# Two column blocks of the output projection accumulated head by head inside the attention loop

## The chip, the core and the metric

One core of one Trainium2 chip runs the whole program. The metric is the device time in microseconds (us), the median over several executions. Engines: PE is the matmul engine, ACT the scalar engine, DVE the vector engine, POOL GpSimd, SP the engine whose queue issues the weight loads.

## What is computed

Two layers of a decoder trunk for 256 tokens of width 2048, all in float32. Each layer is a mixer and a gated ConvFFN, each behind a norm with a learned modulation and added to x through a gate:

```
x = x + gate * mixer(modulate(norm(x)))      # layer 0: NSA (8 heads) and MLA (8 heads)
x = x + gate * conv_ffn(modulate(norm(x)))
x = x + gate * mixer(modulate(norm(x)))      # layer 1: DSA (16 heads, top-k mask)
x = x + gate * conv_ffn(modulate(norm(x)))
mixer(h) = concat(heads) @ w_out             # (256, 2048) @ (2048, 2048)
```

An NSA head is the gated sum of three attentions (compressed, selected, window). The gate and the modulation come from `silu(c) @ ada_w + ada_b`, whose weights are streamed too.

## The kernel before

The program has four sub-layers, n = 0 to 3: even mixer, FFN, odd mixer, FFN. The change touches n = 0 and n = 2.

**Matmuls by weights.** A projection is worked off in units. A unit is 128 rows by 512 columns of a weight, 256 KB, loaded by SP into one of 8 slots of `ring` (`matrix`, L417, by `unit`, L411, which waits until the slot's last unit is used). For precision each factor is split in two: ACT rounds the unit (`high`, L1046) into `ring_hi`, DVE takes the remainder (`low`, L1443) into `ring_lo`, and PE forms hi x hi, lo x hi and hi x lo (`rows_block`, L774): six matmuls of 128x512 per unit, over two tiles of 128 tokens. The left factor is split in the same way, `hT` into `hT_hi` (ACT) and `hT_lo` (DVE, `low_hT`, L1460). All four streams are queues written out by hand; each engine runs its own in order, and they meet at semaphores that count (`hi_ok`, `lo_ok`, `unit_used`, ...).

**Attention.** `pe_attention` (L601), ACT's `attention` (L1159) and DVE's (L1584) run one loop over units: for the even mixer 24 NSA units, three per head (cmp, slc, win), then 8 MLA units; for the odd mixer 16 DSA units, one per head. Step n of the loop holds on PE: query transposes for unit n+1 if it begins a head, logits of n, transposes of the probabilities of n-2, values of n-3. On ACT: copy of the queries, exponentials of n, scaling of n-1, copy of the transposed probabilities of n-2. On DVE: bias, mask and row maximum of n (`logits`), the reciprocal of the sums of n-1 (`weights`), the copy of a finished head (unit n-4) into `hT` (L1623), and in every second step one late unit of the modulation (`rest_unit`, L1422: one operation over 128x2048). PSUM has eight banks; logits (S_B), transposes (T_B), values (O_B) and queries (Q_B) have two each and turn over them, so all eight are used (L588). Before attention starts ACT and DVE have split the first six units of `ev_out` or `od_out` (L1279, L1710).

**Output projection.** After attention all engines wait for the last head, and `out_side` (PE L817, ACT L1121, DVE L1511) follows: ACT and DVE split `hT` pair by pair, and PE works off four blocks of 512 columns, 16 units each, in banks 0 to 3, two banks per block. Between block 0 and block 1 PE spreads the gate row over the partitions (`gate_rows`, L810, banks 4 to 7), which ACT copies back. After each block DVE adds the gated result to x (`residual`, L1498: four operations over 128x512), and ACT squares x for the next norm. The remaining late units of the modulation are spread over blocks 1 and 2 (`more`, L1527). Before the last block PE sums the modulation (`column_sums`, L739), which waits for the last of these units.

## Time and profile before

| | us |
|---|---|
| median of 3 runs | 2169.94 (2161.24 to 2180.1) |
| the profiled execution | 2174.66 |
| its span | 2173.0 |
| busy: PE, DVE, ACT, POOL | 1938.5, 1569.0, 1090.7, 129.2 |
| even attention | 377.7 to 485.0 |
| even output projection | 489.0 to 588.4 |
| odd attention | 1444.0 to 1494.5 |
| odd output projection | 1499.5 to 1598.6 |

The span is what the trace covers; the execution's own time is 1.7 us longer. Busy time of PE includes the modelled drain of its pipelined matmuls. The clock column of a window is the mean clock granted to PE, 1.00 for 2.4 GHz.

### The profile page before, as it was taken

What the parts mean: (1) busy time and instruction counts of PE and PEld (TensorE: products, weight loads), DVE (VectorE), ACT (ScalarE), POOL (GpSimd) and SP (SyncE); (2) the same over time, 40 slices, a digit from 0 to 9 for tenths busy, and PEclk for the clock granted to TensorE, in tenths of its full rate; (3) what the DMA queues carried; (4) which work ended last, traced back from release to release, by engine and by line L of the source; (5) the groups of instructions that cost most, each with busy time, mean ns of one, the idle gap of its engine ahead of it and who ended that gap; (6) DMA issues with size and microseconds to landing.
All of it is one profiled execution on the core that took longest, in us unless ns stands there. A gap on an engine that the chain in (4) does not pass through costs nothing.

```text
span 2173.0 us, 35788 instructions
## 1 busy us (share of the span) xinstructions
PE 1938.5 (89%) x11518; PEld 1684.7 (78%) x11518; DVE 1569.0 (72%) x2443; ACT 1090.7 (50%) x2384; POOL 129.2 (6%) x221
## 2 busy tenths in 40 slices
PE   3189978789899999999998999748989999999998
PEld 2068855567699999997777777636779999998787
DVE  4987743765787878887876767687766777778554
ACT  1145625674455455556454555346545555556443
POOL 1210000000100000000010000000000000000000
PEclk9589979799999999999999999669999999999999
DMA  8979965456588878785985998445757677665565
GB/s 326 401 258 342 328 232 161 155 174 216 172 284 272 278 245 280 255 278 188 327 281 187 331 314 308 137 163 203 251 182 226 221 242 223 221 221 171 178 188 178
DMA packets 210837, 521.47 MB, mean 240 GB/s; under 512 B 24945, under 2 KB 38770, under 8 KB 185874
## 3 DMA queue, kind: packets, MB, share of 16 engines
q1 hardware_dynamic: 180578, 316.17, 45.1%
q0 software_dynamic: 28032, 201.44, 25.1%
q10 hardware_dynamic: 2096, 2.12, 0.3%
q8 instruction: 81, 1.33, 0.2%
q14 instruction: 50, 0.41, 0.1%
HBM read 517.52 MB, written 2.12 MB: 239 GB/s over the span
## 4 chain that ended last, share of the span: by engine, by line
PE 77%; DVE 10%; DMA 6%; ACT 3%; issue 3%; SPq 0%; DVEq 0%; ACTq 0%; POOLq 0%
PE ps L794 12%; PE ps L789 12%; PE ps L790 12%; PE ps L860 11%; PE ps L856 11%; PE ps L857 11%; DVE acc L1381 4%; PE ps L916 2%; DMA first_ring<-in_ada_w 2%; PE ps L648 2%; DVE ring_lo L1449 1%; PE ps L908 1%; DMA ring<-in_ffn_w_down 1%; DMA ring<-in_od_w_in 1%; DMA ring<-in_ffn_w_up 1%
## 5 line engine op out<-in xcount | busy, mean ns | idle before, releaser
L1010 ACT ACTIVATE ring_hi<-ring 128x512 fp32r<-128x512 f32 (+1 forms) x1152 | 696.0, 622 | 657.4 <-DMA ring<-in_ffn_w_up 255.1
L1449 DVE TENSOR_TENSOR ring_lo<-ring,ring_hi 128x512 fp32r<-128x512 f32 (+1 forms) x1152 | 741.6, 679 | 373.4 <-ACT ring_hi L1010 371.5
L856 PE MATMUL ps<-hT_hi,ring_hi 128*128 128x256 f32 x2048 | 513.8, 283 | 5.3 <-issue 4.6
L857 PE MATMUL ps<-hT_lo,ring_hi 128*128 128x256 f32 x2048 | 508.7, 280 | 0.0
L856 PEld LDWEIGHTS ps<-hT_hi,ring_hi 128*128 128x128 f32 x2048 | 386.2, 189 | 6.1 <-issue 5.6
L857 PEld LDWEIGHTS ps<-hT_lo,ring_hi 128*128 128x128 f32 x2048 | 388.7, 190 | 0.0
L860 PE MATMUL ps<-hT_hi,ring_lo 128*128 128x256 f32 x2048 | 330.1, 282 | 1.5 <-issue 1.4
L789 PE MATMUL ps<-ring_hi,hT_hi 128*128 128x512 f32 (+2 forms) x768 | 302.0, 394 | 14.5 <-issue 9.4
L790 PE MATMUL ps<-ring_hi,hT_lo 128*128 128x512 f32 (+2 forms) x768 | 301.0, 393 | 0.0
L860 PEld LDWEIGHTS ps<-hT_hi,ring_lo 128*128 128x128 f32 x2048 | 280.1, 188 | 1.9 <-issue 1.6
L1381 DVE SCALAR_TENSOR_TENSOR acc<-aring,cs_now,acc 128x2048 f32<-128x2048 f32 x106 | 249.3, 2352 | 7.1 <-DMA aring<-in_ada_w 1.2
L794 PE MATMUL ps<-ring_lo,hT_hi 128*128 128x512 f32 (+2 forms) x768 | 238.4, 392 | 3.4 <-DVE ring_lo L1449 3.4
L789 PE MATMUL ps<-ring_hi,act_hi 128*128 128x512 f32 x512 | 202.8, 396 | 5.0 <-issue 5.0
L790 PE MATMUL ps<-ring_hi,act_lo 128*128 128x512 f32 x512 | 201.9, 394 | 0.0
L528 POOL DMA_DIRECT2D aring<-in_ada_w x176 | 93.0, 528 | 1597.2 <-DVE acc L1381 1574.8
L789 PEld LDWEIGHTS ps<-ring_hi,hT_hi 128*128 128x128 f32 x768 | 149.0, 194 | 49.4 <-issue 10.3
L1381 DVE SCALAR_TENSOR_TENSOR acc<-aring,cs,acc 128x2048 f32<-128x2048 f32 x70 | 164.6, 2351 | 12.7 <-DMA aring<-in_ada_w 6.0
L790 PEld LDWEIGHTS ps<-ring_hi,hT_lo 128*128 128x128 f32 x768 | 149.0, 194 | 31.5 <-issue 0.5
L794 PEld LDWEIGHTS ps<-ring_lo,hT_hi 128*128 128x128 f32 x768 | 145.9, 193 | 35.0 <-DVE ring_lo L1449 5.4
L794 PE MATMUL ps<-ring_lo,act_hi 128*128 128x512 f32 x512 | 161.6, 397 | 2.7 <-DVE ring_lo L1449 2.7
L1786 DVE SCALAR_TENSOR_TENSOR cbuf<-ps,cw_now,cbuf 128x255 f32<-128x255 f32 (+1 forms) x256 | 123.5, 482 | 18.2 <-ACT cbuf L1010 9.3
L789 PEld LDWEIGHTS ps<-ring_hi,act_hi 128*128 128x128 f32 x512 | 97.1, 190 | 29.0 <-issue 5.9
(205 smaller groups left out, 1662.6 us busy)
## 6 DMA issues: line engine op xcount, KB each, us to landing
aring<-in_ada_w POOLq DMA_DIRECT2D x176, 1024.0 KB, 6.4
ring<-in_ffn_w_up SPq DMA_DIRECT2D x512, 256.0 KB, 2.9
ring<-in_ffn_w_down SPq DMA_DIRECT2D x256, 256.0 KB, 3.2
ring<-in_od_w_in SPq DMA_DIRECT2D x128, 256.0 KB, 4.6
ring<-in_ev_w_in SPq DMA_DIRECT2D x96, 256.0 KB, 5.6
first_ring<-in_ada_w POOLq DMA_DIRECT2D x16, 1024.0 KB, 7.0
ring<-in_ev_w_out SPq DMA_DIRECT2D x64, 256.0 KB, 3.1
ring<-in_od_w_out SPq DMA_DIRECT2D x64, 256.0 KB, 3.2
```

The costliest lines, as they stand in the source:

```text
L528: pool.dma_start(slot, src).then_inc(landed_, 16)
L648: ins = nc.tensor.matmul(ps[:, b, off:off + nk], l, r, start=j == 0, stop=j == len(parts) - 1)
L789: nc.tensor.matmul(o, hi, w_hi[:, k, :], start=start, stop=False)
L790: nc.tensor.matmul(o, lo, w_hi[:, k, :], start=False, stop=False)
L794: ins = nc.tensor.matmul(ps[:, bank + t, 0:n], hi, w_lo[:, k, :], start=False, stop=stop)
L856: nc.tensor.matmul(o[q], hi, hT_hi[:, kt, :], start=start, stop=False, skip_group_check=True)
L857: nc.tensor.matmul(o[q], hi, hT_lo[:, kt, :], start=False, stop=False, skip_group_check=True)
L860: ins = nc.tensor.matmul(o[q], w_lo[:, k, q * P:(q + 1) * P], hT_hi[:, kt, :], start=False, stop=u == KT - 1, skip_group_check=True)
L1010: ins = nc.scalar.activation(out_, in_, f, **kw)
L1381: put(v.scalar_tensor_tensor(acc[:, t, :], slot, col, acc[:, t, :], ALU.mult, ALU.add), ada_used)
L1449: put(v.tensor_tensor(ring_lo[:, g, part], ring[:, g, part], ring_hi[:, g, part].bitcast(F32), ALU.subtract), lo_ok)
L1786: put(v.scalar_tensor_tensor(cb, u, cw_now[:, s, 1 - tap, gv, q:q + 1], cb, ALU.mult, ALU.add), gconv if (gv == 0 and tap == 1) else None)
```

## The change

Blocks 0 and 1 of each mixer's output projection are no longer formed after attention. Their four output tiles live in banks 0 to 3 during the whole attention loop, and head q's part (units 2q and 2q+1: rows of head q, columns of block 0 and of block 1) is added in step last(q)+5. SP loads the units in that order (`paired`). What attention used two banks for it now does in one: S_B, T_B, O_B, Q_B are 4, 5, 6, 7. A head is split straight from bank O: ACT rounds it (`rounded`, first thing in step last+4) into the place of its own queries, DVE subtracts (`remainder`, same step, after logits) into `hT_lo`; `hT` and `hT_hi` aren't used here any more. ACT's highs for head q stand at the end of step last+3, DVE's lows at the end of step last+4. MLA's rotary queries get a turn of their own in bank Q. Blocks 2 and 3 follow attention, in banks 4, 5 and 0, 1; the gate rows are formed two and two, in banks 6 and 7, before and inside block 2; residuals 0 and 1 run during block 2, and all late units of the modulation that are left lie in block 2. The FFN's projections stay as they are, under the name `down`.

```diff
-            narrow("ev_out", ev_w_out[0], KT)
+            paired("ev_out", ev_w_out[0])
...
-        S_B, T_B, O_B, Q_B = 0, 2, 4, 6
+        S_B, T_B, O_B, Q_B = 4, 5, 6, 7
+        SPLIT_AT, PRODUCT_AT = 3, 5
+        def head_at(att, n, late):
+            return att.qh[n - late] if n - late in att.last_of else None
...
-                if n >= 2:
-                    pe.wait_ge(att.l_ok.handle, n - 1)
+                if n >= 1:
+                    pe.wait_ge(att.l_ok.handle, n)
...
-                if n >= 2:
-                    pe.wait_ge(att.pt_ok.handle, n - 1)
+                if n >= 1:
+                    pe.wait_ge(att.pt_ok.handle, n)
...
-                if first and q >= 2:
-                    pe.wait_ge(att.o_out.handle, q - 1)
+                if first and q >= 1:
+                    pe.wait_ge(att.o_out.handle, q)
...
+                rotary(n + 1)
+                q = head_at(att, n, PRODUCT_AT)
+                if q is not None:
+                    pe.wait_ge(att.o_out.handle, q + 1)
+                    for b in range(2):
+                        product(q, b)
...
+            def heads_out(name, n, att):
+                left = parts_of_heads(att)
+                pe_attention(pe, lane, att, head_product(name, left))
+                gate_rows(n, range(0, 2))
+                rows_block(name, 2 * KT, KT, NB, 4, left, part=(0, 6))
+                pe.wait_ge(gate_ok.handle, 4 * n + 2)
+                gate_rows(n, range(2, 4))
+                rows_block(name, 2 * KT, KT, NB, 4, left, part=(6, KT))
+                pe.wait_ge(gate_ok.handle, 4 * n + 4)
+                column_sums(n + 1)
+                pe.wait_ge(res_out.handle, 4 * n + 1)
+                rows_block(name, 3 * KT, KT, NB, 0, left, part=(0, 6))
+                column_turn(n + 1)
+                rows_block(name, 3 * KT, KT, NB, 0, left, part=(6, KT))
...
+            def heads_out(name, n, next_name):
+                highs(name, 2 * KT, 2 * KT + 4)
+                gate_copies(n, 1, range(0, 2))
+                highs(name, 2 * KT + 4, 2 * KT + 8)
+                gate_copies(n, 2, range(2, 4))
+                run(None, root[:, :], ones[:, 0:1], ACT.Sqrt)
+                highs(name, 2 * KT + 8, 2 * KT + 12)
+                for b in range(2):
+                    act.wait_ge(res_out.handle, 4 * n + b + 1)
+                    x_squares(b)
+                highs(name, 2 * KT + 12, 3 * KT + AHEAD)
...
+                for n in range(len(units) + LAG + 2):
+                    rounded(n)
                     queries(n + 1)
...
+                    rotary(n + 1)
+                    q = head_at(att, n, SPLIT_AT)
+                    if q is not None:
+                        highs(name, 2 * q, 2 * q + 2)
...
-                highs("ev_out", 0, AHEAD)
-                attention(EVA)
+                attention(EVA, "ev_out")
...
+            def heads_out(name, n, next_name):
+                late = len(MOD_REST[n]) - rest_at[n]
+                def more(u0, u1):
+                    for u in range(u0, u1):
+                        low(name, u)
+                        if due(u - 2 * KT, KT, late):
+                            rest_unit(n)
+                more(2 * KT, 2 * KT + 6)
+                residual(name, n, KT, 0)
+                more(2 * KT + 6, 2 * KT + 10)
+                residual(name, n, KT, 1)
+                more(2 * KT + 10, 3 * KT)
+                lows(name, 3 * KT, 3 * KT + 2)
+                residual(name, n, KT, 2)
...
-                for n in range(len(units) + 5):
+                for n in range(len(units) + LAG + 3):
+                    if 0 <= n - 1 < len(units):
+                        weights(n - 1)
                     if n < len(units):
                         logits(n)
-                    if 0 <= n - 1 < len(units):
-                        weights(n - 1)
-                    if 0 <= n - 4 < len(units):
-                        output(n - 4)
+                    remainder(n)
+                    q = head_at(att, n, SPLIT_AT + 1)
+                    if q is not None:
+                        lows(name, 2 * q, 2 * q + 2)
                     if n % every == every - 1:
                         rest_unit(n_sub)
...
-                lows("ev_out", 0, AHEAD)
                 dve.wait_ge(bias_ok.handle, 8)
-                attention(EVA, 0, 2)
+                attention(EVA, "ev_out", 0, 2)
```

## Rows read from the trace of the kernel before

**Rows 1.** The page, part 1: busy us (share of the span) xinstructions.
```profile
PE 1938.5 (89%) x11518; PEld 1684.7 (78%) x11518; DVE 1569.0 (72%) x2443; ACT 1090.7 (50%) x2384; POOL 129.2 (6%) x221
```

**Rows 2.** Windows, even side: PE, PEld, DVE, ACT, POOL busy, PEclk, DMA, GB/s.
```profile
377.70:398.00 20.30, 15.66 (x56) 12.15 (x57) 14.51 (x43) 12.28 (x43) 1.06 (x2) 0.55 0.30 104
398.00:448.50 50.50, 39.62 (x192) 30.95 (x190) 38.01 (x124) 33.12 (x128) 4.75 (x9) 0.83 0.54 180
448.50:485.00 36.50, 33.99 (x194) 25.19 (x194) 23.24 (x58) 26.77 (x88) 3.17 (x6) 0.95 0.44 156
...
489.00:540.20 51.20, 51.15 (x203) 40.24 (x204) 30.44 (x42) 22.94 (x41) 1.23 (x3) 0.94 0.61 209
540.20:588.40 48.20, 47.14 (x214) 36.29 (x213) 31.01 (x43) 24.19 (x42) 5.08 (x5) 1.00 0.61 205
```

**Rows 3.** Windows of odd attention and its first two blocks, same columns.
```profile
1444.00:1458.50 14.50, 11.44 (x58) 10.22 (x59) 10.74 (x29) 9.80 (x31) 1.05 (x2) 0.76 0.30 92
1458.50:1494.50 36.00, 29.61 (x212) 25.88 (x210) 30.27 (x79) 29.18 (x98) 3.17 (x6) 1.00 0.53 184
...
1499.50:1551.30 51.80, 51.72 (x205) 40.48 (x206) 32.71 (x43) 23.13 (x40) 1.75 (x4) 0.94 0.64 214
```

**Rows 4.** Waits in the NSA stretch: total us, times, longest.
```profile
PE ps L662 <- ACT L L1010: 13.6, 10, 2.8
```

**Rows 5.** Timeline of one MLA step on PE: start us, us, engine line op.
```profile
456.02 0.38 PE L615 MATMUL ps<-con,side 128*64 128x128 f32 x2
...
459.71 0.38 PE L615 MATMUL ps<-con,side 128*64 128x128 f32 x2
```

**Rows 6.** Timeline of odd attention, PE and DVE.
```profile
1459.88 0.42 DVE L1604 CUSTOM_DVE_ANT_0 L<-ps,bias 128x256 f32<-128x256 f32 x1 [0.85 <-PE ps L648]
...
1461.42 0.38 PE L621 MATMUL ps<-con,wide 128*128 128x128 f32 x2
...
1462.51 0.33 PE L662 MATMUL ps<-con,L 128*128 128x128 f32 x1
...
1463.72 0.38 PE L621 MATMUL ps<-con,wide 128*128 128x128 f32 x2
```

**Rows 7.** Timeline of DVE: copies of heads 0 and 6.
```profile
399.76 0.42 DVE L1623 COPY hT<-ps 128x256 f32<-128x256 f32 x1
...
442.03 0.42 DVE L1623 COPY hT<-ps 128x256 f32<-128x256 f32 x1
```

**Rows 8.** Timeline of PE in the second block: one unit.
```profile
530.82 0.62 PE L794 MATMUL ps<-ring_lo,hT_hi 128*128 128x512 f32 x2
...
532.21 0.62 PE L794 MATMUL ps<-ring_lo,hT_hi 128*128 128x512 f32 x2
```

**Rows 9.** Timeline: PE's first matmul of the projection.
```profile
489.05 0.76 PE L789 MATMUL ps<-ring_hi,hT_hi 128*128 128x512 f32 x1 [4.16 <-issue]
```

**Rows 10.** Timeline of ACT in odd attention.
```profile
1466.73 0.50 ACT L1010 ACTIVATE L<-L,nmx 128x256 f32<-128x256 f32 x1
...
1467.61 0.79 ACT L1010 ACTIVATE L<-L,rw 128x256 f32<-128x256 f32 x2
1468.30 0.47 ACT L1010 ACTIVATE PT<-ps 128x384 f32<-128x384 f32 x1
1468.67 0.46 ACT L1010 ACTIVATE qT<-ps,gs 128x256 f32<-128x256 f32 x1
```

**Rows 11.** Groups by line, even projection: busy, mean ns, idle before.
```profile
L1449 DVE TENSOR_TENSOR ring_lo<-ring,ring_hi 128x512 fp32r<-128x512 f32 x58 | 38.0, 688 | 30.3 <-ACT ring_hi L1010 30.1
L1010 ACT ACTIVATE ring_hi<-ring 128x512 fp32r<-128x512 f32 x60 | 37.0, 630 | 47.1 <-DMA ring<-in_ev_w_out 45.3 <-DMA ring<-in_ffn_w_up 1.6
L1381 DVE SCALAR_TENSOR_TENSOR acc<-aring,cs,acc 128x2048 f32<-128x2048 f32 x5 | 11.8, 2353 | 0.5
L1506 DVE TENSOR_TENSOR rtmp<-ps,acc 128x512 f32<-128x512 f32 x7 | 4.8, 688 | 7.0 <-PE ps L794 6.6
```

**Rows 12.** Timeline of DVE at the start of even attention.
```profile
377.44 3.69 DVE L1449 TENSOR_TENSOR ring_lo<-ring,ring_hi 128x512 fp32r<-128x512 f32 x6
```

More of the change, by code:

```diff
@@ L447, in narrow, with paired @@
                         matrix(PLAN[name] + units * b, w, units, i * (2 * NB) + b * NB, NB, i * (2 * units))
+            def paired(name, w):
+                for kt in range(KT):
+                    for b in range(2):
+                        g = PLAN[name] + 2 * kt + b
+                        unit(g, g, w[kt * P:(kt + 1) * P, b * NB:(b + 1) * NB], ring[:, g % RING, :])
+                for b in range(2, 4):
+                    matrix(PLAN[name] + KT * b, w, KT, b * NB, NB)
             def up(name, w):
@@ L693, in pe_attention @@
             queries(0)
-            for n in range(len(units) + LAG + 1):
+            for n in range(len(units) + PRODUCT_AT):
                 queries(n + 1)
@@ L786, in rows_block @@
                         for t in range(ST):
-                            o, rows_ = ps[:, bank + t, 0:n], slice(t * P, (t + 1) * P)
-                            hi, lo = (part(u * UK + k)[:, rows_] for part in left)
+                            o = ps[:, bank + t, 0:n]
+                            hi, lo = (x(u * UK + k, t) for x in left)
                             nc.tensor.matmul(o, hi, w_hi[:, k, :], start=start, stop=False)
@@ L808, in in_proj, with gate_rows @@
                 rows_block(name, 2 * KT * pairs, KT, cols - 2 * pairs * NB, 0, h_parts)
-            def gate_rows(n):
+            def gate_rows(n, js=range(4)):
                 pe.wait_ge(ada_used.handle, first_mod(n) + GATE_UNITS[n])
-                for j in range(4):
-                    ins = nc.tensor.matmul(ps[:, 4 + j, :], ones[:, :], acc[:, 2, j * NB:(j + 1) * NB], start=True, stop=True)
+                for j in js:
+                    ins = nc.tensor.matmul(ps[:, (6 + j % 2) if n % 2 == 0 else 4 + j, :], ones[:, :], acc[:, 2, j * NB:(j + 1) * NB],
+                                           start=True, stop=True)
@@ L815, in gate_rows, with head_product, product @@
                 lane.done(ins, gate_red)
-            def out_side(name, n, units, left):
-                rows_block(name, 0, units, NB, 0, left, pairs_before=PAIRS_BEFORE[n, "out"])
-                if n % 2 == 1:
-                    pe.wait_ge(up_pair.handle, 32 * (n // 2 + 1))
+            def head_product(name, left):
+                def product(kt, b):
+                    at, start, stop = 2 * kt + b, kt == 0, kt == KT - 1
+                    w_hi, w_lo = (x[:, (PLAN[name] + at) % RING, :] for x in (ring_hi, ring_lo))
+                    pe.wait_ge(hi_ok.handle, nth(name, at, 0))
+                    for t in range(ST):
+                        hi, lo = (x(kt, t) for x in left)
+                        nc.tensor.matmul(ps[:, 2 * b + t, :], hi, w_hi, start=start, stop=False)
+                        nc.tensor.matmul(ps[:, 2 * b + t, :], lo, w_hi, start=False, stop=False)
+                    pe.wait_ge(lo_ok.handle, nth(name, at, 0))
+                    for t in range(ST):
+                        ins = nc.tensor.matmul(ps[:, 2 * b + t, :], left[0](kt, t), w_lo, start=False, stop=stop)
+                    lane.done(ins, unit_used)
+                return product
@@ L826, in out_side @@
                     if b == 0 or n == 3:
[L827 removed]
+                        rows_block(name, FT * (2 + b), FT, NB, 2 * b, act_parts)
                     else:
@@ L1135, in out_side, with down @@
+            def down(name, n, next_name):
+                units = FT
+                for u in range(units // 2):
+                    act.wait_ge(up_pair.handle, 32 * (n // 2) + turns_for(u))
+                    run(h_hi, act_hi[:, 2 * u:2 * u + 2, :], act_pair(u), ACT.Copy)
+                    if 2 * u >= AHEAD:
+                        highs(name, 2 * u, 2 * u + 2)
+                    if u % 2 == 1 and u < 8:
+                        up_tile(n // 2, 28 + u // 2, u // 2, 1)
                 highs(name, units, units + AHEAD)
-                act.wait_ge(gate_red.handle, n + 1)
@@ L1137, in out_side @@
-                for j in range(4):
-                    run(gate_ok, acc[:, 2, j * NB:(j + 1) * NB], ps[:, 4 + j, :], ACT.Copy)
+                gate_copies(n, 1)
                 if n < 3:
@@ L1169, in queries, with rotary @@
                         act.wait_ge(att.s_ok.handle, att.last_of[q - 2] + 1)
-                    bank = Q_B if kind == "mla" else Q_B + q % 2
                     if kind == "mla":
-                        run(None, qpT[:, q % 2, :], ps[0:ROPE, Q_B + 1, 0:S], ACT.Copy, scale=(HD + ROPE) ** -0.5)
                         run(None, knT[:, q % 2, :], ps[:, Q_B, S:2 * S], ACT.Copy, scale=prm[:, ROWS["nope_g"][0] + 1:ROWS["nope_g"][0] + 2])
                     g = {"dsa": 1, "mla": 2}.get(kind, 0)
-                    run(att.q_ok, qT[:, q % 2, :], ps[:, bank, 0:S], ACT.Copy, scale=gs[:, g:g + 1])
+                    run(att.q_ok, qT[:, q % 2, :], ps[:, Q_B, 0:S], ACT.Copy, scale=gs[:, g:g + 1])
+                def rotary(n):
+                    if n < len(units) and units[n][0] == "mla":
+                        act.wait_ge(att.r_raw.handle, units[n][1] + 1)
+                        run(att.r_ok, qpT[:, qh[n] % 2, :], ps[0:ROPE, Q_B, 0:S], ACT.Copy, scale=(HD + ROPE) ** -0.5)
                 def exps(n):
```

193 lines of the change are left out of this document (111 added, 82 removed).

## The prediction

> **What bounds the kernel now.** The page comes first: the matmul engine, PE, is busy 89% of the span [rows 1], so a gain must come out of time in which PE stands still or runs slowly. Next, the stages by window. Even attention runs from 377.7 to 485.0 us and odd attention from 1444.0 to 1494.5 us. Each output projection follows with four blocks, the first two ending at 540.2 and 1551.3 us. Over the blocks PE is busy 47 to 51 us of each 48 to 52 [rows 2, 3], so there the matmul work itself is the bound. Over attention PE is busy 15.66 of 20.3, 39.62 of 50.5 and 33.99 of 36.5 us (even), 11.44 of 14.5 and 29.61 of 36.0 us (odd). The clock granted is 0.55 in the first stretch and 0.83 in the second; the two levels are 1.2 and 2.4 GHz, so a third of the second stretch ran at the lower one. The holes are therefore in the 24 NSA units (three per head); with the 8 MLA units PE hardly stands.
>
> The waits say what ends the holes: in the NSA stretch PE waits 13.6 us, ten times, for ACT's scaled probabilities [rows 4]. At 2.4 GHz one step of the pipeline takes PE 3.69 us in MLA [rows 5] and 2.30 us in odd attention, from one head's query transposes (1461.42) to the next's (1463.72) [rows 6]. The NSA steps come from DVE's copies of finished heads: head 0 at 399.76, head 6 at 442.03, so 7.05 us per head [rows 7].
>
> **What the work costs.** A unit of a block takes 1.39 us (530.82 to 532.21) [rows 8]; a head's product, two units, takes 2.77 us, and 16 heads 44.3 us per projection. The same matmuls run either way, so moving them saves only what falls into PE's holes, plus the hand-over. Today PE stands 4.16 us before the first unit at 489.05 [rows 9] and the first two blocks have a mean clock of 0.94, which is about 3 us of slow running in 51.2 [rows 2]. The odd side is alike [rows 3]. So 7 us per projection go for certain, because the product follows attention with no rounding of the whole hT in between. Beside each product ACT gets two highs (0.63 busy, about 0.55 apart: 1.1 us) and the rounding of the head, bounded by 0.36 (the step from PT at 1468.30 to qT at 1468.67, [rows 10]) and 0.63 (a high); I take 0.37. DVE gets two lows, 0.688 each less overlap: 1.3 us, and the remainder, which replaces the copy of about 0.42 and costs the same (bounds 0.4 and 0.69) [rows 7, 11].
>
> **Even attention, step by step.** Each engine runs its queue in order. I followed the waits of the new code, with durations from the steps shown [rows 5, 6, 10]. PE's odd step divides into queries and logits, 1.09 (1461.42 to 1462.51), and transposes and values, 1.21 (to 1463.72); by the number of operations I split these into 0.22 and 0.87, 0.5 and 0.7. NSA's parts are a little shorter, having no mask matmuls. Per unit: DVE's two logits reductions 0.65 (0.42 for the wider, at 1459.88, and about half of it for the other), ACT's exponentials 0.89 (1466.73 to 1467.61), its scaling 0.70, the copy 0.37, a semaphore about 0.08. Two things are new. With one bank O, PE's first values of a head wait for DVE's remainder of the head before, which waits for ACT's rounded copy, and in ACT's queue this stands behind the two highs. With one bank T, PE's transposes wait for one more copy. From the end of one product to the end of the next, in NSA: queries 0.22, PE logits 0.93, DVE logits 0.72, exponentials 0.98, scaling 0.70, copy 0.30, highs 1.10, rounded 0.37, remainder 0.49, values 0.70, logits 0.73, transposes 0.44, values 0.64, product 2.77: 11.1 us. Against 7.05 + 2.77 = 9.8 us apart, each such head loses 1.3 us instead of gaining. In MLA the chain is remainder 0.5, values 0.66, rotary 0.22, product 2.77, queries 0.66, logits 2.3, DVE logits 0.7: 7.8 us against 3.69 + 2.77 = 6.5.
>
> The sum: six steps before the first product 22 us; 6 heads x 11.1 = 66.6; the eight MLA steps 51 (four at 7.8, the earlier ones with two products and two waits 19.8); the tail with five products 17.5; less 1.2, because six lows of 3.69 us no longer stand ahead of DVE's first logits [rows 12]. That is 155.9, and the gate rows (four matmuls, 3.6 us by both orders) make 159.5. Before, 377.7 to 540.2 is 162.5. So 3 us come out here, at full clock.
>
> But before, a third of the NSA stretch was at 1.2 GHz, and PE still has holes of 1 to 1.5 us in that chain. If the clock drops there, a product costs up to 2.77 more: bounds 0 and 6 x 2.77 = 17 us. I take 5, by the third (17/3). The Trainium skill, TensorE: Matmul & The Clock Gate, A second HAM failure mode, says that cycling PSUM banks with small idles between matmul groups makes the clock swing; by it the upper bound would be the nearer. The rows agree that it swings in this stage: 0.55, 0.83, 0.95 [rows 2].
>
> **Odd attention.** Here every unit is a head, so each step carries a product. The chain: remainder 0.5 after DVE's logits, values 0.66, product 2.77, queries 0.22, logits 1.1, DVE logits 0.65: 5.9 us, against 2.30 + 2.77 = 5.07 of pure PE work. Five steps without product 14.5, then 3.1 + 10 x 5.9 = 62, the tail 21: 97.5, with gate rows 101.1. Before, 1444.0 to 1551.3 is 107.3. So 6 us come out.
>
> **The third block (block 2).** The late units of the modulation (5 even, 6 odd, 2.353 us each on DVE) were spread over two blocks and now lie in one [rows 11]. In its 22.2 us DVE has 16 lows 11, those units 11.8 or 14.1, and two residuals of 4 x 0.688 = 2.7 each: 28 or 31 us. DVE can begin about 5 us ahead, at the tail of attention, but residual 0 waits for the last product, and the ring of 8 units limits the lead. ACT's second gate copies now stand in the middle of the block, and its squares wait for residual 1. I count PE standing 5 us (even) and 7 us (odd), with the column sums behind the last unit; before, the last two blocks together hold PE up 1 us (48.2 - 47.14, [rows 2]). Net loss 4 and 6 us. Bounds for both together: 0 if the lead holds, 18 if there is none (DVE's excess over PE, 6 and 8, and 2 each for the copies).
>
> **Sum.** Even -3 + 5 + 4 = +6, odd -6 + 6 = 0. With the unknowns leaning both ways I take +5 us. The profiled execution took 2174.7 us (span 2173.0), 4.7 above the median of 2169.9; so 2179.7 there, and as a median 2174 to 2175. I say 2174. The measurement can tell about 1%, 22 us; this lies within it.
>
> **Where rules pull.** The Trainium skill, Perfetto Trace Analysis, Optimization Strategy, holds that interleaving stages with different bounds may pay; MLA and odd attention, at 93 and 82% PE, are hardly a different stage. The same page, Matmuls, wants matmul groups to rotate through PSUM banks so that evacuation overlaps; the change takes that away, and what it costs is in the chains above.
>
> **Rivals.** *The holes are filled* (faster): the steps do not lengthen as I chain them, because highs run before ACT is needed and PE, denser, keeps 2.4 GHz. For: PE's holes plus slow running in NSA are large (its busy 55.3 us at a mean clock of 0.75 is 42 us of work at full clock in a stretch of 70.8). Then a head takes 9.3 instead of 11.1 (-11) and keeps the clock (-5), the start at 0.55 improves by 4, and the third blocks stall 3 instead of 12 (-9): -29 from my sum, 2145. Against: ACT is already the releaser of PE [rows 4]. Chance 0.2.
>
> *One bank each is the bound* (slower): the hand-over PE to DVE to ACT to PE through single banks, with 2.353 us modulation units of DVE in its middle, and a clock that falls in the holes. Place: NSA products. Price: the clock term at 17 instead of 5 (+12), two of three such units falling inside the chain, 6 heads x 1 us (+6), and the third blocks at 18 instead of 12 (+6): 2198. It decides from about 13 us per NSA head on. For: PE's wait for ACT [rows 4], and the clock of 0.55 and 0.83 [rows 2]. Chance 0.24.
>
> *The order does not do what it says*: weights arrive late, since two units per 6 to 11 us replace a full ring at the start of the block. Against: 256 KB per unit in a few us and DMA far from full (share 0.30 to 0.54, [rows 2]). Then the products cost more, and it is a part of the second rival. My forecast has 0.56.
>
> **How the numbers follow.** Range: 2146 to 2197. It reaches to the first rival's time and to the second's, so that about half of either's chance, 0.22 in all, lies outside; my sum's own bounds, with the clock term from 0 to 17 and the third blocks from 0 to 18, are 2157 to 2192. Under 2148.2 is faster by over 1%, above 2191.6 slower: 0.20, 0.56, 0.24 come from the three cases.
>
> **What would show it.** Between two products about 11 us in NSA, 7.8 in MLA, 5.9 in odd attention; the waits naming DVE's remainder (hT_lo) ahead of PE's values, and ACT's rounded copy behind highs; a first block end near 542 to 547 and attention with two blocks near 101 us on the odd side; in the third block DVE busy nearly throughout with PE waiting for ring_lo for some us. If NSA products stand 9.5 us apart at clock 1.0, the first rival is right; at 13 and more with a clock at 0.8, the second. Wrong altogether if the hand-over hole of 4 us stays.

## The result and the profile after

The changed kernel takes 2194.7 us (median of four runs, 2186.5 to 2197.8) beside 2170.8 for the kernel before in the same comparison. The ratio is 1.0112, with a 95% interval of 1.0075 to 1.0149: slower, by about 1%, and the interval is clear of no change. The forecast was 2174, with a range of 2146 to 2197. The range holds the time, near its upper end; the case called the likeliest, no change to speak of, is not the one that came.

The page, part 1 (busy us, share of the span, instructions; its span is 2191.0), against [rows 1]:

```profile
PE 1949.1 (89%) x11518; PEld 1684.6 (77%) x11518; DVE 1555.7 (71%) x2427; ACT 1087.9 (50%) x2400; POOL 129.2 (6%) x221
```

PE's share is the same, but it is 11 us busier with the same 11518 instructions, so some of them ran slower. The windows say where (columns as in [rows 2]). Even side: up to the first product, five NSA products, MLA, the tail, blocks 2 and 3. Odd side: up to the first product, the products, blocks 2 and 3:

```profile
375.75:400.96 25.21, 18.46 (x71) 13.82 (x71) 15.16 (x53) 15.17 (x53) 1.58 (x3) 0.64 0.35 116
400.96:469.80 68.84, 56.18 (x223) 43.57 (x221) 38.83 (x109) 35.58 (x125) 3.94 (x8) 0.75 0.44 149
469.80:522.88 53.08, 46.85 (x185) 32.43 (x183) 19.59 (x56) 27.94 (x86) 1.85 (x4) 0.72 0.32 109
522.88:557.70 34.82, 32.81 (x164) 25.71 (x162) 24.52 (x39) 18.43 (x47) 2.11 (x4) 1.00 0.62 206
557.70:614.23 56.53, 52.78 (x225) 39.35 (x223) 36.45 (x47) 27.53 (x51) 6.14 (x7) 0.97 0.66 218
1463.96:1484.28 20.32, 13.96 (x80) 11.23 (x81) 12.19 (x37) 16.08 (x50) 1.05 (x2) 0.88 0.31 104
1484.28:1562.76 78.48, 71.08 (x388) 58.72 (x387) 50.58 (x105) 48.32 (x133) 4.23 (x8) 1.00 0.62 197
1562.76:1618.20 55.44, 52.02 (x224) 37.92 (x223) 41.00 (x50) 28.27 (x52) 2.11 (x4) 1.00 0.75 243
```

The clock column stands out. The NSA stretch went from 0.83 [rows 2] to 0.75, and the MLA stretch, once 0.95 [rows 2], to 0.72. In the tail of even attention (522.88 to 557.70), and in all of the odd products, it is 1.00.

From here on a side's length is the time from its first query transpose to the end of the last matmul of blocks 0 and 1, without the gate rows. In the kernel before, the gate rows stand between block 0 and block 1 and keep the next unit waiting for 3.0 us:

```profile
514.04 3.60 PE L814 MATMUL ps<-acc,ones 128*128 128x512 f32 x8
517.07 0.79 PE L789 MATMUL ps<-ring_hi,hT_hi 128*128 128x512 f32 x1
```

Block 1 ends at 539.73 and at 1550.40, so before the change the even side is 539.73 - 377.76 - 3.03 = 158.9 us and the odd side 1550.40 - 1442.82 - 3.03 = 104.6. (The prediction took 540.2, 1551.3 and 3.6 us of gate rows, each up to 1 us too much.) After, they are 557.70 - 375.75 = 182.0 and 1562.76 - 1463.96 = 98.8. So the even side lost 23.1 us and the odd side gained 5.8. Blocks 2 and 3, less the gate rows now inside them (2.6 us), take 53.9 and 52.8 against 48.6 (to 588.35) and 48.1 (to 1598.54): a loss of 5.2 and 4.7. With 0.8 us less of gate rows that is +26.4 in all. The two spans differ by 18.0, because the first stage ended 2.0 us earlier, the stretch between the two sides took 4.7 us less and the last FFN 1.7 less. Stages that no edit touches vary by as much from profile to profile (numbers at e3), so these are not put down to the change.

PE's timeline shows NSA products 13.8 us apart (456.13 to 469.80 is 13.7), and then 22.3 and 22.7 us over three steps each, MLA steps but for one:

```profile
456.13 0.99 PE L885 MATMUL ps<-ring_hi,wide_r 128*128 128x512 f32 x1
...
469.80 0.99 PE L885 MATMUL ps<-ring_hi,wide_r 128*128 128x512 f32 x1
...
492.11 0.67 PE L885 MATMUL ps<-ring_hi,wide_r 128*128 128x512 f32 x1
...
514.79 0.78 PE L885 MATMUL ps<-ring_hi,wide_r 128*128 128x512 f32 x1
```

Inside one product (same view) the clock changes while it runs:

```profile
428.69 0.99 PE L885 MATMUL ps<-ring_hi,wide_r 128*128 128x512 f32 x1
...
429.90 0.63 PE L885 MATMUL ps<-ring_hi,wide_r 128*128 128x512 f32 x1
...
431.38 0.40 PE L885 MATMUL ps<-ring_hi,wide_r 128*128 128x512 f32 x1
```

The first unit runs mostly at 1.2 GHz (0.63 us per matmul; 2.69 us to the second unit's start, at a mean granted clock of 0.56), the second at 2.4 GHz (0.40, at 1.00). The logits and values that follow stand behind waits, and at the next product the lower level is back.

The waits name the hand-overs (us in total, times, longest): first over 376 to 470 us, then over 470 to 515 us.

```profile
ACT qT L1097 <- PE ps L655: 16.9, 6, 3.4
...
PE ps L709 <- ACT PT L1097: 9.3, 7, 1.4
...
PE ps L724 <- DVE hT_lo L1760: 6.9, 6, 1.2
```

```profile
PE ps L653 <- ACT qpT L1097: 4.9, 4, 2.0
```

The ACT row is ACT waiting for PE's query transposes, not PE. The first PE row is the one bank T (PE may not overwrite the transposes before ACT has copied them), the second the one bank O (a head's first values behind DVE's remainder), and in MLA PE waits for ACT's copy of the rotary queries in the one bank Q. In blocks 2 and 3 PE waited 3.3 us (even) and 2.2 us (odd) for a low.

### The profile page after: what moved, and what is told of

It reads as the page before. It is cut to its first block, busy times and chain, and to the rows that moved or that the text cites. A ratio compares the mean times of both kernels' runs of the same rounds, so it can differ in the third digit from the quotient of the medians.

```text
span 2191.0 us, 35407 instructions
## 1 busy us (share of the span) xinstructions
PE 1949.1 (89%) x11518; PEld 1684.6 (77%) x11518; DVE 1555.7 (71%) x2427; ACT 1087.9 (50%) x2400; POOL 129.2 (6%) x221
## 4 chain that ended last, share of the span: by engine, by line
PE 77%; DVE 10%; DMA 6%; ACT 3%; issue 2%; SPq 0%; DVEq 0%; ACTq 0%; POOLq 0%
PE ps L951 11%; PE ps L947 11%; PE ps L948 11%; PE ps L853 10%; PE ps L849 10%; PE ps L850 10%; DVE acc L1499 4%; PE ps L695 2%; DMA first_ring<-in_ada_w 2%; PE ps L1007 2%; PE ps L885 1%; PE ps L886 1%; PE ps L999 1%; DVE ring_lo L1567 1%; PE ps L889 1%
## 5 line engine op out<-in xcount | busy, mean ns | idle before, releaser
L850 PE MATMUL ps<-ring_hi,hT_lo 128*128 128x512 f32 (+2 forms) x640 | 247.9, 388 | 0.0
L849 PE MATMUL ps<-ring_hi,hT_hi 128*128 128x512 f32 (+2 forms) x512 | 196.5, 385 | 3.7 <-ACT ring_hi L1097 3.7
L1499 DVE SCALAR_TENSOR_TENSOR acc<-aring,cs,acc 128x2048 f32<-128x2048 f32 x70 | 164.6, 2351 | 13.3 <-DMA aring<-in_ada_w 6.1
L853 PE MATMUL ps<-ring_lo,hT_hi 128*128 128x512 f32 (+2 forms) x512 | 155.8, 386 | 1.2 <-DVE ring_lo L1567 1.2
L850 PEld LDWEIGHTS ps<-ring_hi,hT_lo 128*128 128x128 f32 x640 | 123.0, 192 | 25.7 <-issue 1.0
L849 PEld LDWEIGHTS ps<-ring_hi,act_hi 128*128 128x128 f32 x512 | 97.2, 190 | 29.2 <-issue 5.8
L853 PEld LDWEIGHTS ps<-ring_lo,act_hi 128*128 128x128 f32 x512 | 96.0, 188 | 27.8 <-DVE ring_lo L1567 5.5
L849 PEld LDWEIGHTS ps<-ring_hi,hT_hi 128*128 128x128 f32 x512 | 98.5, 192 | 24.1 <-ACT ring_hi L1097 5.5
```

Of the source, the lines that this page charges most:

```text
L849: nc.tensor.matmul(o, hi, w_hi[:, k, :], start=start, stop=False)
L850: nc.tensor.matmul(o, lo, w_hi[:, k, :], start=False, stop=False)
L853: ins = nc.tensor.matmul(ps[:, bank + t, 0:n], left[0](u * UK + k, t), w_lo[:, k, :], start=False, stop=stop)
L1499: put(v.scalar_tensor_tensor(acc[:, t, :], slot, col, acc[:, t, :], ALU.mult, ALU.add), ada_used)
```

## The experiments

Each ran beside the kernel before. The lengths are as defined above. They come from one profiled execution of each kernel, which lies up to 11 us from its median (e1: 2214.6 beside 2225.7), so a few us between two sides should not be leaned on.

| run | even, us | odd, us | median, us | ratio to before (95%) |
|---|---|---|---|---|
| before | 158.9 | 104.6 | 2170.8 | 1 |
| after | 182.0 | 98.8 | 2194.7 | 1.0112 (1.0075 to 1.0149) |
| e1 | 193.3 | 112.8 | 2225.7 | 1.0273 (1.0205 to 1.0340) |
| e5 | 193.5 | 110.4 | 2220.7 | 1.0245 (1.0189 to 1.0301) |
| e6 | 172.5 | 104.4 | 2199.5 | 1.0132 (1.0075 to 1.0189) |
| e9 | 169.1 | 104.2 | 2192.4 | 1.0108 (1.0074 to 1.0141) |
| e2 | 176.1 | 99.3 | 2193.2 | 1.0098 (1.0070 to 1.0125) |
| e3 | 166.8 | 99.7 | 2188.2 | 1.0082 (1.0057 to 1.0107) |
| e4 | 158.3 | 101.9 | 2176.6 | 1.0047 (1.0018 to 1.0077) |
| e7 | 160.1 | 87.1 | 2163.4 | 0.9983 (0.9957 to 1.0010) |
| e12 | 146.4 | 88.4 | 2152.0 | 0.9924 (0.9891 to 0.9957) |
| e8 | 142.0 | 91.4 | 2151.0 | 0.9920 (0.9891 to 0.9949) |
| e10 | 145.5 | 91.5 | 2154.4 | 0.9925 (0.9897 to 0.9953) |
| e11 | 152.2 | 97.0 | 2162.3 | 0.9971 (0.9945 to 0.9996) |

### Products or banks? (e1)

```diff
-                q = head_at(att, n, PRODUCT_AT)
-                if q is not None:
-                    pe.wait_ge(att.o_out.handle, q + 1)
-                    for b in range(2):
-                        product(q, b)
+            pe.wait_ge(att.o_out.handle, len(att.last_of))
+            for q in range(len(att.last_of)):
+                for b in range(2):
+                    product(q, b)
...
+                highs(name, AHEAD, 2 * KT)
...
+                lows(name, AHEAD, 2 * KT)
```

With the products, ACT's highs and DVE's lows of these units leave the loop too, as the last two lines say: six units are split ahead of it, the rest behind it.

> The changed kernel, but the products of blocks 0 and 1 are all formed after the attention loop (six units split ahead, the rest after), as in the kernel before; single banks, the rotary turn of its own, head-by-head split from bank O and the rest of the projection stay. Theory A (single banks and the rotary turn stretch the steps by themselves): even attention without any product is longer than the 107 us of before, its MLA steps 5 us and more instead of 3.7, NSA heads above 8 us instead of 7.05, odd attention above 55 instead of 50.5; the whole at 2190 or above. Theory B (the products in the middle of the steps do it, single banks cost little): attention takes 107 and 51 us as before, the clock in MLA is back at 0.95, and only the third blocks' loss is left: 2178 to 2182.

Theory A, at 2225.7 us. PE's first product matmul on the even side:

```profile
523.66 0.79 PE L884 MATMUL ps<-ring_hi,wide_r 128*128 128x512 f32 x1 [0.93 <-DVE hT_lo L1759]
```

From the first query transpose (376.38) to here are 147.3 us, without a single product among the steps; the kernel before takes 111.3 (377.76 to 489.05, [rows 9]). The odd side takes 65.8 against 56.7. By the query transposes NSA heads are 9.9 us apart (394.00 to 453.64 over six) and MLA steps 7.7 to 8.3 us (466.82, 474.54, 482.25, 490.50, 498.74). The windows (NSA, then MLA; PE, PEld, DVE, ACT, POOL busy, PEclk, DMA, GB/s) show the clock in MLA at 0.62:

```profile
403.00:453.60 50.60, 41.05 (x163) 31.38 (x162) 32.78 (x104) 30.26 (x117) 4.23 (x8) 0.70 0.45 150
453.60:510.00 56.40, 48.06 (x169) 31.02 (x167) 17.90 (x52) 27.14 (x88) 2.12 (x4) 0.62 0.26 90
```

The other half of the reading is as important: with the products among the steps the two sides are 11.3 and 14.0 us shorter than with them behind (182.0 against 193.3, 98.8 against 112.8). The move itself, of products and splits together, pays. What was given up to make room for it costs 34.4 us on the even side (193.3 against 158.9), more than it brings, and 8.2 on the odd side (112.8 against 104.6), less than it brings.

### Which banks? (e5, e6, e9)

In e1 banks 0 to 3 are free during attention, so they can be given back to one user at a time.

```diff
-                q, b = qh[n], S_B
+                q, b = qh[n], (S_B, 0)[n % 2]
...
-                b = T_B
+                b = (T_B, 1)[n % 2]
```

> The run with all products after attention (even: 147 us from the first query transposes to the first product matmul, odd 66, against 111 and 55.5 in the kernel before), but the logits and the transposed probabilities have two banks each again (4 and 0, 5 and 1); values and queries keep one. If the single banks of logits and probabilities stretched the steps, even falls from 147 to below 125 and odd to below 60. If the values' and queries' hand-overs do it, both stay within 5 us of 147 and 66.

```profile
519.06 0.80 PE L884 MATMUL ps<-ring_hi,wide_r 128*128 128x512 f32 x1 [0.93 <-DVE hT_lo L1759]
```

519.06 - 371.52 = 147.5 us: nothing on the even side. The odd side takes 63.2 instead of 65.8.

```diff
-                o = ps[:, O_B, 0:S]
+                ob = (O_B, 2)[q % 2]
+                o = ps[:, ob, 0:S]
...
+                b = Q_B if kind == "mla" or q % 2 == 0 else 3
+                if q >= (1 if kind == "mla" else 2):
+                    pe.wait_ge(att.q_ok.handle, q if kind == "mla" else q - 1)
...
-                    ins = nc.tensor.transpose(ps[0:ROPE, Q_B, t * P:(t + 1) * P],
+                    ins = nc.tensor.transpose(ps[0:ROPE, 3, t * P:(t + 1) * P],
```

> The same run with all products after attention, but the values and the queries have two banks each again (6 and 2, 7 and 3; the rotary queries in the second one, without a turn of their own in the first); logits and probabilities keep one. My theory for the changed kernel (PE waits for DVE's remainder before a head's first values, and in MLA for ACT's qpT) says that this run loses most of the stretch: even from 147 to below 125, odd from 66 to below 60, the MLA clock back above 0.9. If not, it is the logits' or the probabilities' bank.

```profile
503.79 0.50 PE L887 MATMUL ps<-ring_hi,wide_r 128*128 128x512 f32 x1 [0.93 <-DVE hT_lo L1762]
```

128.1 us (from 375.73) and 59.6: it takes 19 of the 36 us. On the even side that is less than was expected (below 125), and the MLA clock came to 0.83 (448 to 489 us), not above 0.9; the odd side is below 60 as expected.

The third kernel of this group (e9) makes both edits.

> The run with all products after attention and two banks for each of logits, probabilities, values and queries, as in the kernel before; what is left of the change in attention is the split of a head straight from its bank and DVE's order (reciprocal of the sums before the logits). One bank of each cost 147 us (even) and 66 (odd) up to the first product, the kernel before takes 111 and 55.5; two banks for values and queries gave 128 and 60. If the banks are all of the stretch, this run gives 111 to 114 and 56 to 57. If the head's split and DVE's order have a part of their own, it stays at 120 and more, or 59 and more.

```profile
498.76 0.50 PE L887 MATMUL ps<-ring_hi,wide_r 128*128 128x512 f32 x1 [2.10 <-DVE hT_lo L1762]
```

124.3 us (from 374.44) and 57.8. So on the odd side the banks are nearly all of it, and on the even side 13.0 us are left that are no bank's. Most of them are neither of the two that I had named, the head's split and DVE's order. The timeline of e9 in MLA, PE and ACT:

```profile
458.21 0.38 PE L667 MATMUL ps<-con,side 128*64 128x128 f32 x2
...
459.54 0.47 ACT L1099 ACTIVATE PT<-ps 128x384 f32<-128x384 f32 x1
459.91 0.37 ACT L1099 ACTIVATE qpT<-ps 64x256 f32<-64x256 f32 x1
...
460.38 0.67 PE L697 MATMUL ps<-knT,qT 128*128 128x256 f32 x2 [1.35 <-issue]
```

PE transposes the rotary queries (L667) as the last thing of a step, and the logits of the very next step need them; ACT copies them (qpT) behind its exponentials, scaling and PT, until 460.28. PE stands 1.35 us, until 460.38 (the profile names no releaser, "issue"; the copy is what ends just before). In the kernel before the same transposes stood at the start of a step (456.02, [rows 5]), one step ahead of their logits. MLA steps are 5.27 us apart here (463.92 - 458.65) against 3.69, both at a clock of 1.00. The six steps from 448.19 to 479.72 take 31.5 us, the same six before 22.2 (449.01 to 471.23): 9.3 of the 13.0 us. The other 3.7 lie ahead of these steps and behind them, and were not taken apart.

With the table this splits the even side: the new places in the queues cost 169.1 - 158.9 = 10.2 us (the hand-over to the projection, shorter now, is in it), the single banks 193.3 - 169.1 = 24.2, and the products among the steps give 11.3 back: +23.1. On the odd side it is -0.4, +8.6 and -14.0: -5.8. The medians bear the banks' part out: 2225.7 - 2192.4 = 33.3 us for 24.2 + 8.6. The split holds for this order of taking things away; in another order the parts could come out otherwise.

### ACT's highs ahead of the exponentials (e2)

```diff
                     queries(n + 1)
+                    q = head_at(att, n, SPLIT_AT)
+                    if q is not None:
+                        highs(name, 2 * q, 2 * q + 2)
                     if n < len(units):
                         exps(n)
```

> The changed kernel, but ACT's two highs of a head stand before the exponentials of their step, no longer at its end, where the next head's rounded copy is queued behind them. If the copy behind the highs is what stretches a head (my chain counts 1.10 us for it), NSA products come 12.6 us apart instead of 13.7 and odd ones below 5.85, the whole 5 to 10 us less: 2185 to 2189. If the chain runs over ACT's exponentials anyway (the highs only change their place in it), the distances stay at 13.7 and 5.85 and the time is the same within 3 us.

NSA products come 12.7 us apart ((471.52 - 408.09) / 5), as the chain said, and the even side is 5.9 us shorter. Odd steps stay at 5.85, which had been expected to fall, and the median fell by 1.5 us where 5 to 10 were expected. The highs are a part of the NSA chain and no large one.

### The rotary queries ahead (e3)

The transposes of heads 2(n-1) and 2(n-1)+1 stand in steps n = 1 to 4, in banks 0 to 3, and ACT copies them into a part of `wide` that is free.

```diff
-                if n >= len(units) or units[n][0] != "mla":
+                if att is not EVA or not 1 <= n <= 4:
                     return
-                for t in range(ST):
-                    ins = nc.tensor.transpose(ps[0:ROPE, Q_B, t * P:(t + 1) * P],
+                for e in range(2):
+                    h = 2 * (n - 1) + e
+                    for t in range(ST):
+                        ins = nc.tensor.transpose(ps[0:ROPE, n - 1, e * S + t * P:e * S + (t + 1) * P],
```

> The changed kernel, but MLA's rotary queries are transposed and copied in steps 1 to 4 through banks 0 to 3, before these hold products, so that in MLA bank Q has one turn per head. Theory A (the second turn in the one bank Q makes PE wait for ACT's copy and the clock fall): the three MLA steps without product between two products shrink from 22.5 us towards 3 x 3.7 plus a product, 14 to 16 us, at a clock above 0.85; 12 to 20 us less in all, 2175 to 2183. Theory B (PE waits in MLA for the other single banks, the turn only comes first): the next hand-over takes its place, 3 to 5 us less, 2190 to 2192. The NSA part stays at 13.7 us per head in either.

Windows of the NSA products and of MLA up to the first MLA head's product:

```profile
402.65:470.77 68.12, 55.46 (x223) 42.93 (x221) 38.47 (x109) 35.21 (x124) 3.95 (x8) 0.75 0.43 149
470.77:509.29 38.52, 34.82 (x170) 25.40 (x169) 19.42 (x56) 25.38 (x80) 1.85 (x4) 0.93 0.44 150
```

The MLA stretch takes 38.5 us instead of 53.1, at 0.93 instead of 0.72; the gaps of 22.3 and 22.7 are 15.3 and 16.1. NSA is as it was. That is theory A at its place. The even side is 15.2 us shorter than 182.0, but the median fell only by 6.5, short of the 12 to 20 expected. Stages that no edit touches vary by some us from profile to profile (over these runs the first FFN from its column sums to its gate rows 460.0 to 466.9, the odd mixer ahead of its attention 313.0 to 324.6). In this profile they lay high (465.9 and 324.6), but whether that is so in the other executions is not shown.

### A product in two steps (e4)

```diff
+                q = head_at(att, n, PRODUCT_AT + 1)
+                if q is not None:
+                    product(q, 1)
                 q = head_at(att, n, PRODUCT_AT)
                 if q is not None:
                     pe.wait_ge(att.o_out.handle, q + 1)
-                    for b in range(2):
-                        product(q, b)
+                    product(q, 0)
```

> The changed kernel, but a head's product for block 1 is formed one step after that for block 0, not behind it, so that each step gets 1.39 us of it and not every third 2.77 us. Theory A (what is late are the hand-overs through single banks; the product only lies between them): PE's work falls into waits of two steps instead of one, NSA heads shrink from 13.7 by up to 1.4 us, and the clock in NSA rises a little above 0.76; 4 to 8 us less. Theory B (the product is the work that the chain waits for): no change in NSA, within 3 us; in odd attention every step has the same 2.77 us either way, so nothing is to be seen there.

```profile
400.69:460.00 59.31, 51.30 (x243) 41.30 (x242) 40.32 (x119) 37.90 (x135) 4.23 (x8) 0.86 0.57 193
460.00:498.00 38.00, 32.58 (x156) 22.23 (x155) 17.89 (x46) 24.71 (x77) 1.59 (x3) 0.91 0.33 113
```

18 us less by the medians, where I had allowed 4 to 8. NSA products are 10.9 us apart instead of 13.8 ((455.19 - 400.69) / 5), by more than the 1.4 us that a hand-over could hide: the clock rose with it, from 0.75 to 0.86 in NSA and from 0.72 to 0.91 in MLA. The odd side, which has a product in every step anyway, got 3 us longer by its extra step.

### Products where PE waits (e7, e12, e8)

```diff
                     output(n - LAG)
+                q = head_at(att, n, PRODUCT_AT + 1)
+                if q is not None:
+                    product(q, 1)
+                q = head_at(att, n, PRODUCT_AT)
+                if q is not None:
+                    pe.wait_ge(att.o_out.handle, q + 1)
+                    product(q, 0)
                 if 0 <= n - LAG - 1 < len(units):
                     values(n - LAG - 1)
                 rotary(n + 1)
-                q = head_at(att, n, PRODUCT_AT)
-                if q is not None:
-                    pe.wait_ge(att.o_out.handle, q + 1)
-                    for b in range(2):
-                        product(q, b)
```

> As the run with a head's two products in two steps, and both now stand between the transposes and the values of their step, where PE waits for DVE's remainder of the next head. If that wait is what a step of odd attention has beyond its work (5.85 against 2.30 + 2.77 = 5.07), odd steps fall to about 5.1 and the odd side by some 9 us, MLA steps by 0.5 or more: 2160 to 2168 in all. If the chain takes the product along in any place (the values only come later, and with them ACT's rounded copy), steps stay at 5.85 and the time at 2174 to 2179.

The window over all odd products:

```profile
1465.10:1533.98 68.88, 68.88 (x394) 59.56 (x392) 53.26 (x112) 49.97 (x140) 4.22 (x8) 1.00 0.70 228
```

PE is busy 68.88 of 68.88 us and a step takes 4.85 instead of 5.85: the wait for DVE's remainder lies wholly under the product. Two places in a queue, the only difference from e4, were worth 14.8 us on this side (101.9 to 87.1; 11.7 against the changed kernel). The even side did not get shorter against e4 (160.1 and 158.3), so the 0.5 us per MLA step that was expected did not come.

> The best run so far without its third edit: rotary queries ahead and products in two steps before the values, but in steps last+5 and last+6. From the first query transposes to the last product the even side took 160.1 us with the products before the values alone and 142.0 in the best run. If the rotary queries ahead are what gave these 18 us (they gave 14.7 to the changed kernel), this run takes 142 to 146 us there and 2150 to 2156 in all; if it was the placing of the second half in the step with the wait, 152 us and more, and 2158 to 2163.

146.4 us and 2152.0: as expected of the rotary queries, together with e7. Over the NSA products (403.84 to 458.85) the clock is 0.90, and heads are 11.0 us apart. The last kernel of this line (e8) adds one edit to it, `SPLIT_AT, PRODUCT_AT = 4, 6`.

> Three edits together: rotary queries transposed ahead in steps 1 to 4, products in two steps and before the values, and all of it one step later (last+6 and last+7), so that in NSA the second half of a product stands in the very step in which PE waits for the remainder. If waits for hand-overs are filled by this, NSA products come about 10 us apart, the MLA gaps of 14 to 22 us shrink to about 12, odd steps to 5.1: 2145 to 2158, below the kernel before. If the clock stays down in NSA and MLA, the even side keeps its length and the time lies at 2165 to 2175.

Windows over the even side, to the first product, NSA, MLA with tail, and over the odd products:

```profile
377.24:405.59 28.35, 22.17 (x95) 17.40 (x95) 16.38 (x53) 19.43 (x68) 1.59 (x3) 0.69 0.33 112
405.59:454.90 49.31, 40.05 (x218) 30.98 (x216) 37.24 (x112) 33.34 (x118) 4.24 (x8) 1.00 0.59 203
454.90:519.20 64.30, 62.91 (x327) 48.61 (x326) 44.57 (x92) 44.02 (x124) 3.71 (x7) 1.00 0.60 204
...
1449.63:1517.69 68.06, 66.83 (x377) 57.57 (x376) 52.75 (x107) 47.66 (x131) 4.24 (x8) 1.00 0.71 232
```

With single banks throughout, the clock is 1.00 from the first product on, NSA products are 10.3 us apart ((456.85 - 405.59) / 5), odd steps 4.85, and the even side takes 142.0 us, 16.9 less than before the change. The MLA gaps are 13.3 and 14.1 us (456.85, 470.15, 484.21), not the 12 expected. The kernel is 0.8% faster than the kernel before (interval 0.5 to 1.1%), and by the two ratios 1.9% faster than the changed one. Between e12 and e8 there is nothing to tell in the whole: 4.4 us less on the even side, 3.0 more on the odd one, by its extra step.

### DVE's order and the late units (e10, e11)

```diff
-                    if 0 <= n - 1 < len(units):
-                        weights(n - 1)
                     if n < len(units):
                         logits(n)
+                    if 0 <= n - 1 < len(units):
+                        weights(n - 1)
```

> The best run so far (rotary queries ahead, products in two steps before the values, one step later), and DVE takes a step's logits before the reciprocal of the step before again, the order of the kernel before. If DVE's logits are held up by ACT's exponentials through the new order, NSA heads come below 10 us apart and the even side is 3 to 8 us shorter: 2143 to 2149. If the new order matters to nobody (ACT needs the reciprocal for its scaling at once), or even helps, there is no gain, or a loss of up to 5 us: 2150 to 2156.

2154.4, the even side 3.5 us longer and the odd one as it was: DVE's new order costs nothing that these runs can tell.

```diff
-                    if n % every == every - 1:
+                    if n % every == every - 1 or n in ((0, 2, 4, 32, 34) if att is EVA else (0, 2, 4, 6, 16, 18)):
                         rest_unit(n_sub)
```

> The best run so far, and the five (even) and six (odd) late units of the modulation that lay in block 2 are done by DVE inside attention, in the steps before the first products and behind the last heads. The third blocks then have no such unit: if these units are what holds PE up there (PE waits for the lows and for the last unit, 3.7 us even and 3.8 odd on each side), blocks 2 and 3 take 49 to 50 us without the gate rows on either side instead of 52 and 51, and the whole is 4 to 7 us shorter: 2144 to 2147. If DVE's time is missed in attention instead, the steps before the first product grow by as much: 2150 to 2156.

```profile
377.25:409.29 32.04, 23.84 (x94) 17.96 (x95) 22.86 (x56) 19.16 (x68) 3.17 (x6) 0.62 0.58 197
409.29:462.40 53.11, 44.23 (x217) 34.16 (x215) 38.12 (x112) 33.70 (x119) 4.22 (x8) 0.90 0.57 189
```

2162.3, worse than either expectation. From the last product to the column sums it takes 28.3 and 27.4 us instead of 31.4 and 29.2, so the units do cause that stall, 4.9 us of it. But the sides grew by 10.2 and 5.6: the first product of the even side comes 3.7 us later (32.0 against 28.4), with three more units of 2.35 us ahead of it, and the clock over the NSA products then stood at 0.90 where e8 has 1.00.

## Why the prediction was right or wrong

**Right: the odd side.** The steps come every 5.85 us (1490.13 to 1495.98) for a forecast of 5.9, and the side takes 98.8 us for 97.5. The gain of 6 is 5.8. The chain was the stated one: PE waits 7.4 us, eleven times, for DVE's remainder, and once a product lies under that wait (e7) the step is PE's own work, 4.85 us, a little under the 5.07 worked out for it. (The 2.30 us in that 5.07 was read from a step in which PE does not wait; the next one, from 1463.72 to 1467.36, takes 3.64 with a wait of 1.22. As PE's own work the figure is right.)

**Right: the third blocks.** A loss of 4 and 6 us was stated, 5.2 and 4.7 came. The sum is right; that the odd side would lose more is not. That the late units are behind half of it, 4.9 us, e11 shows; the rest was not taken apart.

**Wrong: "the earlier ones 19.8", the MLA steps without a product taken at 3.69.** By the query transposes (478.37, 485.83, 495.40, 501.10, 507.91, 518.62) they take 7.46, 5.70 and 6.81 us, and the two with an NSA head's product 9.57 and 10.71. The eight steps come to 61.3 us (478.37 to 539.71) for 51 forecast: the first four take 29.5 for 19.8, the last four 31.8 for 31.2. The prediction put two NSA products into the first four; only one stands there, so the miss is not in the count of products. A part of it is the clock, 0.72 in this stretch. Two causes are separate from each other. The rotary turn puts the transposes one step too close to their logits, 1.58 us a step even with two banks and at full clock (e9). And in the single bank Q the next head's transposes wait for the same copy (1.97 us at 478.12). I had costed the new rotary turn by PE's own 0.22 us and had not asked what it waits for, or how long before its use it now stands. Taking it out gave 15.2 us on the even side (e3), the clock's rise from 0.72 to 0.93 included.

**Wrong in size: the clock term, +5.** Steps 0 to 23 take 102.6 us (375.75 to 478.37) for 22 + 66.6 - 1.2 = 87.4 in the sum at full clock: +15.2 where I took 5, near the upper bound of 17. The clock was 0.64 and 0.75 there. That the slow clock is most of it, and not a chain mis-added, is what e4 and e8 speak for: the same single banks give 10.9 us per head at 0.86 and 10.3 at 1.00. No run kept the changed order at a full clock, so how much of 13.8 - 11.1 is clock alone stays open. The 10.2 us beyond the term and the 9.7 of the first MLA steps are nearly the whole miss on the even side (182.0 for 155.9 + 5).

The page TensorE: Matmul & The Clock Gate of the Trainium skill, section A second HAM failure mode, names cycling through PSUM banks with small idles between matmul groups as a cause of a swinging clock. I had weighed that rule and then sided with a third of the bound. The rows agree that the clock fell, 0.95 to 0.72 in MLA, but attention turned over fewer banks when it did. Nor does the sum of the idles decide it here: over its NSA products PE stands 12.7 of 68.8 us in the changed kernel, at 0.75, and 9.3 of 49.3 in e8, nearly the same share, with the same single banks, at 1.00. What sets the clock in these stretches stays open.

**The sum.** Even +23.1 for +2, odd -5.8 for -6, third blocks +9.9 for +10, gate rows -0.8 for 0: 26.4 for 6. By the medians it is 23.9. That the time still lies in the range, 2 us inside its end, is owed to the range reaching to the second rival's time, not to the sum: the sum's own bounds ended at 2192.

**The rivals.** "One bank each is the bound" (2198) was the nearer story: its point of decision, 13 us per NSA head, is passed at 13.8, and its place and its clock are right. It missed that MLA would fall too; its 18 us for the third blocks did not come, and what DVE's late units cost inside the chain was not measured by itself. "The holes are filled" (2145) is not what this kernel does, but e8 does it in 2151. "The order does not do what it says" did not occur: no wait of PE in even attention or among the odd products names the weights, and among the odd products ACT waited for them 6.8 us, three times, at a pace of PE that was the forecast one.

The Perfetto Trace Analysis page of the Trainium skill, section Matmuls, wants matmul groups to rotate through banks. The runs agree: here the rotation is worth 24.2 us on the even side and 8.6 on the odd (e1 against e9), if nothing is put into the waits.

## What to carry to other kernels

Before work is moved into a pipeline, ask of every hand-over that loses its second buffer what its engine can do meanwhile, and put the moved work exactly there: ahead of the waiting instruction, in small pieces, not behind it. When a step is cut out of another (here the rotary queries), count how many steps lie between it and its use, in every queue that it passes, and not only its duration. And do not cost a falling clock low when the change adds waits to a stretch whose clock already swings: here it took 15.2 us of a bound of 17, if the sum around it was right.

## What the hardware showed that was not expected

A low clock can last through a long stretch and look like work. Six MLA steps without any product, the same matmuls but for one record, in the kernel before, in e9 and in e1 (columns as in [rows 2]):

```profile
449.01:471.23 22.22, 22.22 (x132) 16.03 (x131) 12.02 (x39) 18.16 (x61) 1.58 (x3) 1.00 0.43 152
...
448.19:479.72 31.53, 23.64 (x132) 16.19 (x131) 13.02 (x39) 19.24 (x65) 1.59 (x3) 1.00 0.30 104
...
458.88:504.94 46.06, 40.85 (x133) 25.84 (x132) 13.27 (x38) 20.34 (x64) 1.59 (x3) 0.56 0.21 69
```

In e1 PE is busy 40.85 us, 89% of the stretch, with what it does in 22.22 us before. So a full PE in us is no sign that it is well used; the clock column has to be read beside it.

Standing still does not by itself bring the clock down: in e9 PE stands 7.9 of the 31.5 us at 1.00, in e1 5.2 of 46.1 at 0.56. A busy share of about 81% goes with very different clocks too: 56.18 of 68.84 us at 0.75 (after), 40.05 of 49.31 at 1.00 (e8). With the same products in two pieces instead of one the clock was 0.86 instead of 0.75 (e4). No run shows which property of the order makes the difference.
